# Second feed-forward product of a two-layer hybrid decoder trunk: one block product at a time over the whole depth, kept in PSUM, with the activations' operand sums made in stage one

## The chip, the core and the metric

The kernel runs on one core of a Trainium2 chip. Its time is the device time of one execution in microseconds (us). Three runs of the kernel before gave 3005.19, 3008.79 and 3010.06 us, a median of 3008.79. The execution that the profiler recorded took 3007.68 us, of which the profile's span covers 3005.6.

The engines are named as the profile names them: PE is TensorE, the matrix engine (PEld its weight loads), DVE is VectorE, ACT is ScalarE, POOL is GpSimd, SP is SyncE, which here issues all DMA transfers. PSUM is the memory in which PE accumulates, in eight banks of 128 x 512 f32; SBUF is the on-chip memory for everything else.

## The reference

Two layers. Each mixes three head groups (latent attention, a state space scan, a recurrent unit), attends to 256 memory tokens, and ends with a squared-ReLU feed-forward part. Only that part is changed:

```
DEPTH, SEQ, D_MODEL, D_FF = 2, 1024, 1024, 4096
hm = rms_norm(x, mlp_norm_g[l]) @ w_mlp1[l]          # (1024, 1024) @ (1024, 4096)
x  = x + jnp.square(jax.nn.relu(hm)) @ w_mlp2[l]     # (1024, 4096) @ (4096, 1024)
...
return rms_norm(x, final_norm_g)                     # after the last layer
```

Everything is f32. x is held transposed, as 8 tiles of 128 rows by 1024 tokens. An f32 product is formed from three: each operand is split into a high part, which ACT makes by a copy to fp32r, and a low part, which is the operand less its high part, and high x high, high x low and low x high are accumulated.

## The kernel before

Both feed-forward products go by Strassen's scheme in Winograd's form. A product of 2 x 2 blocks takes seven block products (M1, M2, M7, M5, M6, M4, M3 in the order of execution, `P_M1` to `P_M3` in the code) in place of eight, and pays with sums of blocks before and after. Block 11 of the result is M1 + M2, and the others are M1 with sums and differences of the rest. The weights' side of M7 and the following products is S3, S1, S2, A22 and S4, where S3 = A11 - A21, S1 = A21 + A22, S2 = A22 - S3, S4 = A12 - S2 (as the code forms them); the activations' side has the same chain of four sums.

**Stage one** (first product, `for f in range(1, NFP)`) goes through 15 pairs of hidden tiles after a first pair that is done plainly. A pair is seven products of 12 matmuls (L1514). For each pair SP loads four weight blocks (L627), ACT makes high parts (L1949), POOL makes low parts (L887) and the four weight sums (L893), DVE combines the seven results (L2548) and applies relu and the norm factor (`hidden`, L2486), ACT squares (L1937), and SP stores the four squared blocks of 128 x 512 (L632).

**Stage two** (second product) goes through seven panels of 512 hidden rows with all seven products each, and through an eighth panel plainly (16 units of 12 matmuls, L1605). A product of a panel is four units of six matmuls (L1588), and each unit fills one PSUM bank. Only M2 stays in PSUM, in banks 0 to 3, for all panels. The other six products of every panel go through banks 4 to 7, and DVE adds each of their units, 128 x 512, to accumulators in SBUF (`add_unit`, L2491: z1, z7, z5, z6, and x itself), so that the bank can be filled again. The operands of a product stand in one of four slots (`a_op`, `b_op`). To fill one, ACT makes the two high parts (L1976, L1989), DVE the activations' low part (L2510) and POOL the weights' low part (L922), each 128 x 1024; DVE also forms the activations' four sums of a panel (L2514) and POOL the weights' four (L927). Near the end POOL and DVE fold the accumulators together and into x (L974, L2596).

What sets the order is the order of the code on each engine, which is written out by hand. An engine goes through its own list and stops at each `wait_ge` until a semaphore has the number. PE waits for `x_add` (DVE has emptied the bank) and for `a_lo` and `b_lo` (the operands are there); ACT waits for `u_done` (PE is through with the slot) and for the sums.

Of the kernel before, what the change touches and what calls it, by code (L numbers as in the profile page):

```python
# [26 lines left out]
P = 128  # L27
DEPTH = 2
# [19 lines left out]
LAST = NFB - 1  # L48
# [7 lines left out]
W1_SUMS = 4 * (NFP - 1)  # L56
SLOTS = 4
FILL_SLOT = (0, 1, 2, 3, 0, 1, 2)
LATE_SLOT = (0, 1, 2, 3, 0, 2, 3)


def slot_of(b, i):

    return (LATE_SLOT if b == LAST - 1 else FILL_SLOT)[i]


def fills_done(b, i):

    return b * NPR + i + 1


def units_before(b, p):

    return (b * NPR + p) * 4


def slot_units(b, i):

    s = slot_of(b, i)
    before = [(bb, p) for bb in (b - 1, b) if bb >= 0 for p in range(NPR) if (bb, p) < (b, i) and slot_of(bb, p) == s]  # L80
    return units_before(*before[-1]) + 4 if before else None


def adds_before(b, p):

    x_products = (P_M4, P_M3)
    kept = sum((24 if m else 8) for m in range(b))
    return kept + 4 * sum(q != P_M2 and (b > 0 or q in x_products) for q in range(p))


PLAIN_A = ((0, 0), (0, 1), (2, 0), (2, 1))
PLAIN_B = ((1, 0), (3, 0), (1, 1), (3, 1))
PLAIN_B_ORDER = (0, 2, 1, 3)


def plain_units(slot):

    return max(units_before(LAST - 1, p) + 4 for p in range(NPR) if slot_of(LAST - 1, p) == slot)


def units_waited(n):

    return LAST * 24 + n - 19
# [4 lines left out]
LAST_ADDS = adds_before(LAST, 0)  # L108
LAST_UNITS = units_before(LAST, 0)
# [106 lines left out]
def x_tile(n):  # L216
# [51 lines left out]
def trunk(nc, xT, memT, posb, ropec, small, final_g, wt, wv, wh, lruw, outT):  # L268
# [10 lines left out]
    with ctx:  # L279
# [2503 lines left out]
```

## Time and profile before

| | us |
|---|---|
| median of three runs | 3008.79 |
| the profiled execution | 3007.68 |
| its span | 3005.6 |
| PE busy | 2824.3 (94%) |
| DVE busy | 1738.5 (58%) |
| POOL busy | 1596.1 (53%) |
| ACT busy | 1129.2 (38%) |
| stage one, two layers | 296.21 and 298.50 |
| stage two, two layers | 394.44 and 399.41 |

PE runs in order and is the busy engine nearly everywhere, so the span is what PE takes: its matmuls at their pitch, its idle time, and the stretches in which its granted clock is below 1.00. The busy time of a line counts overlapping matmuls once. In the rows, "idle before <- X" names the work whose end let the engine go on.

### The profile page before, as it was taken

How to read it: one execution, taken by the hardware profiler on the slowest of the kernel's cores; microseconds unless marked ns; L12 is line 12 of the kernel's file. 1: busy time of each engine (PE TensorE's matmuls, PEld its weight loads, DVE VectorE, ACT ScalarE, POOL GpSimd, SP SyncE). 2: the span in 40 equal slices, each digit the busy share in tenths (PEclk: the TensorE clock that was granted, in tenths of full speed). 3: DMA queues.
4: the chain of work that ended last, by engine and by line, in shares of the span. 5: the costliest groups of instructions: out<-in, count | busy, mean ns of one | idle time of the engine just before them, and what ended most of it. 6: DMA issues, size and time to landing. Idle time of an engine off the chain costs nothing.

```text
span 3005.6 us, 33919 instructions
## 1 busy us (share of the span) xinstructions
PE 2824.3 (94%) x12958; PEld 2192.6 (73%) x12958; DVE 1738.5 (58%) x1775; ACT 1129.2 (38%) x1762; POOL 1596.1 (53%) x897
## 2 busy tenths in 40 slices
PE   8999999999999988888999999999999999888887
PEld 6766668887788877666787566788787888766665
DVE  8574465034733357989776644630446333598987
ACT  3455543242433333222215655422414333422233
POOL 4334433422577776666633345234136777766666
PEclk9999999999999999999999999999999999999999
DMA  3100011310133342222110000113011333423221
GB/s 130 47 14 1 15 43 49 106 56 28 45 110 113 113 140 98 70 98 84 56 55 33 14 1 15 56 57 112 29 39 60 109 111 110 146 78 105 70 98 56
DMA packets 96298, 208.27 MB, mean 69 GB/s; under 512 B 11280, under 2 KB 13328, under 8 KB 95504
## 3 DMA queue, kind: packets, MB, share of 16 engines
q1 hardware_dynamic: 96144, 206.18, 20.3%
q8 instruction: 101, 1.65, 0.2%
q14 instruction: 53, 0.43, 0.0%
HBM read 168.13 MB, written 38.01 MB: 69 GB/s over the span
## 4 chain that ended last, share of the span: by engine, by line
PE 65%; DVE 20%; POOL 7%; ACT 3%; issue 2%; DMA 2%; SPq 0%; DVEq 0%; POOLq 0%; ACTq 0%
PE ps L1018 16%; PE ps L1514 12%; PE ps L1588 9%; PE ps L1386 6%; DVE raw_b L2514 6%; DVE b_op L2510 5%; PE ps L1240 4%; POOL ring L887 3%; PE ps L1270 2%; POOL raw L893 2%; PE ps L1442 2%; PE ps L1605 2%; PE ps L1466 2%; PE ps L1256 2%; DVE z L2491 2%
## 5 line engine op out<-in xcount | busy, mean ns | idle before, releaser
L1588 PE MATMUL ps<-b_op,a_op 128*128 128x512 f32 x2352 | 579.8, 409 | 109.0 <-DVE x L2491 59.2
L1588 PEld LDWEIGHTS ps<-b_op,a_op 128*128 128x128 f32 x2352 | 464.8, 199 | 223.7 <-DVE x L2491 64.2
L1018 PE MATMUL ps<-hA,wsp 128*128 128x512 f32 x1920 | 443.1, 392 | 0.1
L721 POOL TENSOR_TENSOR wsp<-raw,ones 128x1024 fp32r<-128x1024 f32 x63 | 125.9, 1999 | 570.8 <-PE ps L1018 454.9
L1018 PEld LDWEIGHTS ps<-hA,wsp 128*128 128x128 f32 x1920 | 360.3, 188 | 80.9 <-issue 6.2
L922 POOL TENSOR_TENSOR a_op<-raw_a,a_op 128x1024 fp32r<-128x1024 f32 x102 | 282.7, 2772 | 224.6 <-ACT a_op L1989 217.0
L887 POOL TENSOR_TENSOR ring<-raw,ring 128x512 fp32r<-128x512 f32 x210 | 272.9, 1299 | 150.4 <-ACT ring L1949 140.9
L1514 PE MATMUL ps<-hT,ring 128*128 128x512 f32 x1440 | 337.3, 394 | 16.1 <-POOL ring L887 16.1
L1514 PEld LDWEIGHTS ps<-hT,ring 128*128 128x128 f32 x1440 | 273.0, 190 | 76.7 <-POOL ring L887 19.5
L1976 ACT ACTIVATE b_op<-raw_b 128x1024 fp32r<-128x1024 f32 x98 | 103.5, 1056 | 424.3 <-DVE raw_b L2514 279.3
L1514 PE MATMUL ps<-hB,ring 128*128 128x512 f32 x1080 | 250.2, 389 | 0.8 <-POOL ring L887 0.8
L1949 ACT ACTIVATE ring<-raw 128x512 fp32r<-128x512 f32 x210 | 131.9, 630 | 274.7 <-POOL raw L893 205.0
L2510 DVE TENSOR_TENSOR b_op<-raw_b,b_op 128x1024 fp32r<-128x1024 f32 x98 | 219.2, 2247 | 26.3 <-ACT b_op L1976 26.2
L1514 PEld LDWEIGHTS ps<-hB,ring 128*128 128x128 f32 x1080 | 202.5, 188 | 43.6 <-issue 1.6
L927 POOL TENSOR_TENSOR raw_a<-raw_a,raw_a 128x1024 f32<-128x1024 f32 x56 | 181.5, 3241 | 4.4
L2514 DVE TENSOR_TENSOR raw_b<-raw_b,raw_b 128x1024 f32<-128x1024 f32 x56 | 182.7, 3263 | 1.0
L732 POOL TENSOR_TENSOR wsp<-raw,wsp 128x1024 fp32r<-128x1024 f32 x45 | 107.8, 2396 | 137.5 <-ACT wsp L1876 134.5
L1386 PE MATMUL ps<-hA,wsp 128*128 128x512 f32 x768 | 178.1, 391 | 0.8 <-ACT wsp L1876 0.7
L2280 DVE TENSOR_REDUCE nmx<-ps 128x1 f32<-128x256 f32 (+7 forms) x128 | 96.7, 757 | 132.9 <-PE ps L1243 130.9
L2548 DVE TENSOR_TENSOR mu<-mu,ps 128x512 f32<-128x512 f32 x90 | 61.8, 687 | 189.1 <-PE ps L1514 187.1
L724 POOL TENSOR_TENSOR wsp<-raw,wsp 128x1024 fp32r<-128x1024 f32 x63 | 166.2, 2638 | 4.9
L1386 PEld LDWEIGHTS ps<-hA,wsp 128*128 128x128 f32 x768 | 143.6, 188 | 32.7 <-issue 3.2
(326 smaller groups left out, 4592.4 us busy)
## 6 DMA issues: line engine op xcount, KB each, us to landing
raw<-in_weight_tiles SPq DMA_DIRECT2D x108, 512.0 KB, 3.3
hidden_tiles<-hm_s SPq DMA_DIRECT2D x128, 256.0 KB, 2.0
raw_a<-in_weight_tiles SPq DMA_DIRECT2D x64, 512.0 KB, 3.9
raw_b<-hidden_tiles SPq DMA_DIRECT2D x64, 512.0 KB, 5.4
raw<-in_weight_tiles SPq DMA_DIRECT2D x120, 256.0 KB, 3.1
outT<-x SPq DMA_DIRECT2D x16, 256.0 KB, 2.2
x<-in_xT SPq DMA_DIRECT2D x3, 1024.0 KB, 9.6
wh<-in_head_weights SPq DMA_DIRECT2D x8, 256.0 KB, 2.7
```

The lines of the kernel that those rows point to most:

```text
L721: pool.tensor_tensor(wsp[:, s, 0, :], raw[:, s, :], ones[:, 0:1].to_broadcast([P, TILE]), ALU.mult).then_inc(w_ready[s], 1)
L724: pool.tensor_tensor(wsp[:, s, 1, :], raw[:, s, :], wsp[:, s, 0, :].bitcast(F32), ALU.subtract).then_inc(w_ready[s], 1)
L887: pool.tensor_tensor(ring[:, FILL_SLOT[i], 1, :], blk(src), ring[:, FILL_SLOT[i], 0, :].bitcast(F32), ALU.subtract).then_inc(a_lo, 1)
L922: pool.tensor_tensor(op[:, 1, :, :], raw_t[:, :, :], op[:, 0, :, :].bitcast(F32), ALU.subtract).then_inc(a_lo, 1)
L927: pool.tensor_tensor(raw_a[out][:, :, :], raw_a[x0][:, :, :], raw_a[x1][:, :, :], op).then_inc(a_sum, 1)
L1018: last = pe.matmul(ps[:, 2 * buf + half, 0:n], w[:, k, col:col + P], rhs(part, k, half * n, n), start=(at_k == 0 and w is w_hi and part == 0),
L1386: last = pe.matmul(ps[:, 2 * (g % 2) + half, :], w[:, part, k, :], hA[:, a, k, half * HT:(half + 1) * HT], start=(k == 0 and part == 0 and ...
L1514: last = pe.matmul(ps[:, M_BANK[p], :], w[:, part, k, :], rhs(a, k), start=(k == 0 and part == 0 and a == 0), stop=(k == 3 and part == 1))
L1588: last = pe.matmul(ps[:, bank, :], w[:, part, q // 2, r, (q % 2) * P:(q % 2 + 1) * P], h[:, a, r, :], start=(r == 0 and part == 0 and a == ...
L1949: act.activation(ring[:, FILL_SLOT[i], 0, :], blk(src), ACT.Copy).then_inc(a_hi, 1)
L2510: dve.tensor_tensor(op[:, 1, :, :], raw_b[src][:, :, :], op[:, 0, :, :].bitcast(F32), ALU.subtract).then_inc(b_lo, 1)
L2514: dve.tensor_tensor(raw_b[out][:, :, :], raw_b[x0][:, :, :], raw_b[x1][:, :, :], ALU.subtract).then_inc(b_sum, 1)
```

## The change

Stage two is turned inside out. The loop over the seven products is now the outer one and the loop over panels the inner one, over all eight panels; there is no plain panel any more. A step n is one product of one panel, p, s = divmod(n, 8), and has 24 matmuls in four banks. All eight steps of a product accumulate in the same four banks: M1, M7, M6 and M3 in banks 4 to 7, M2, M5 and M4 in banks 0 to 3. Only when the eighth step is done does DVE add the 128 x 2048 result to the blocks of x that it belongs to (`block_add`; 13 such adds, and 4 of 128 x 512 for M3, `unit_add`). The accumulators z and the folds are gone. The last two steps of M3 are done bank by bank.

The operands come otherwise too. The activations' four sums are made in stage one, on DVE, from the squared blocks of a pair of 128 x 512 (`pair_sums`), and stored: seven blocks of each pair go to memory in place of four, three squared ones and four sums. Stage two loads the operand of a step as it is, 512 KB. The weights' sums move from POOL to DVE (`operand_sum`, one in each step of M7, M5, M6 and M3): a chain through kept blocks, for which a weight block of 512 KB is loaded in every step and two in those of M5, each in two transfers with runs of 256 columns. POOL makes the weights' low parts only. The four slots remain, and the last two steps have slots of their own.

At the start of stage one ACT makes the first two weight blocks' high parts ahead of the norm factor and of the four copies of `high_sums(0)`, which stood in front of them.

```diff
-                    for b in range(LAST):
-                        for p in range(NPR):
-                            panel_product(b, p)
+                    for n in range(RING_FILLS):
+                        p, s = step(n)
+                        operands_ready(n)
+                        if s == 0 and p == 0:
+                            pe.wait_ge(p1_kept, here(p1_kept, NFP - 1))
+                            pe.wait_ge(c_add, here(c_add, NPR * (NFP - 1) - 4))
+                            pe.wait_ge(hm_sq, here(hm_sq, 4 * NFP - 2))
+                        elif s == 0 and p == 1:
+                            pe.wait_ge(hm_sq, here(hm_sq, 4 * NFP))
+                        elif s == 0:
+                            pe.wait_ge(x_add, here(x_add, adds_before(p - 1)))
+                        for q in range(4):
+                            last = operand_products(n, q)
+                        last.then_inc(u_done, 1)
...
+                    def pair_sums(f):
+                        dve.wait_ge(hm_sq, here(hm_sq, 4 * f + 4))
+                        if f:
+                            dve.wait_ge(ht_st, here(ht_st, 64 * f))
+                        b11, b12, b21, b22 = (hms[k][:, cols_of(half)] for k in range(2) for half in range(2))
+                        dve.tensor_tensor(hts[0][:, :], b22, b12, ALU.subtract).then_inc(ht_sum, 1)
+                        dve.tensor_tensor(hts[1][:, :], b12, b11, ALU.subtract).then_inc(ht_sum, 1)
+                        dve.wait_ge(ht_sum, here(ht_sum, 4 * f + 2))
+                        dve.tensor_tensor(hts[2][:, :], b22, hts[1][:, :], ALU.subtract).then_inc(ht_sum, 1)
+                        dve.wait_ge(ht_sum, here(ht_sum, 4 * f + 3))
+                        dve.tensor_tensor(hts[3][:, :], b21, hts[2][:, :], ALU.subtract).then_inc(ht_sum, 1)
...
+                    def block_add(p, i):
+                        out, before = X_BLOCKS[p][i]
+                        bank = 4 * (1 - p % 2)
+                        dve.wait_ge(u_done, here(u_done, STEPS * (p + 1)))
+                        if before:
+                            dve.wait_ge(x_add, here(x_add, before))
+                        dve.tensor_tensor(out, ps[:, bank:bank + 4, :], out, ALU.add).then_inc(x_add, 1)
...
+                    for n in range(2, FILLS):
+                        if n + 1 < FILLS and step(n + 1)[0] in OPERAND_SUMS:
+                            operand_sum(n + 1)
+                        operand_low(n)
+                        p, i = step(n - SLOTS + 1 - STEPS)
+                        if n >= STEPS + SLOTS - 1 and i < X_ADDS[p]:
+                            block_add(p, i)
...
+                    for n in range(SLOTS, FILLS):
+                        sp.wait_ge(b_lo, here(b_lo, n - SLOTS + 1))
+                        load_hidden(n)
+                        sp.wait_ge(a_lo, here(a_lo, W1_FILLS + n - SLOTS + 1))
+                        if n == 6:
+                            sp.wait_ge(ht_st, here(ht_st, 64 * NFP))
+                        load_weights(n)
...
                     high_sums(2)
-                    high_sums(0)
-                    rstd_of(N_MLP, D, 4, rs[:, :]).then_inc(bc_done, 1)
                     w1_high(0, S_A11, 0)
                     w1_high(0, S_A12, 1)
+                    rstd_of(N_MLP, D, 4, rs[:, :]).then_inc(bc_done, 1)
+                    high_sums(0)
```

Three places show how the lists of the engines change. The first is DVE in stage one, from the last product of a pair to the middle of the next. Before (mu are the kept parts of the combination, ps are PSUM banks):

```order
L2548 TENSOR_TENSOR ps<-mu_54,ps 128x512
L2486 SCALAR_TENSOR_TENSOR ps<-ps,rs 128x512
L2548 TENSOR_TENSOR ps<-mu_54,ps 128x512
L2486 SCALAR_TENSOR_TENSOR ps<-ps,rs 128x512
L2548 TENSOR_TENSOR mu_54<-mu_54,ps 128x512
```

The same place after the change (hm_s are the squared blocks, hm_t the four sums):

```order
L2415 TENSOR_TENSOR ps<-mu_60,ps 128x512
L2346 SCALAR_TENSOR_TENSOR ps<-ps,rs 128x512
L2354 TENSOR_TENSOR hm_t_62<-hm_s_117,hm_s_116 128x512
L2355 TENSOR_TENSOR hm_t_63<-hm_s_116 128x512
L2357 TENSOR_TENSOR hm_t_64<-hm_s_117,hm_t_63 128x512
L2359 TENSOR_TENSOR hm_t_65<-hm_s_117,hm_t_64 128x512
L2415 TENSOR_TENSOR ps<-mu_60,ps 128x512
L2346 SCALAR_TENSOR_TENSOR ps<-ps,rs 128x512
```

Four sums have come between the last `hidden` of a pair and the first combination of the next.

The second place is SP's list for one pair of stage one. Before (hidden_tiles is the store in memory, raw the weight blocks):

```order
L627 DMA raw<-in_weight_tiles 128x512 x3
L632 DMA hidden_tiles<-hm_s_106 128x512
L627 DMA raw<-in_weight_tiles 128x512
L632 DMA hidden_tiles<-hm_s_107 128x512 x2
L632 DMA hidden_tiles<-hm_s_106 128x512
```

After:

```order
L612 DMA raw<-in_weight_tiles 128x512 x2
L623 DMA hidden_operands<-hm_t_62 128x512
L623 DMA hidden_operands<-hm_t_63 128x512
L623 DMA hidden_operands<-hm_t_64 128x512
L623 DMA hidden_operands<-hm_t_65 128x512
L612 DMA raw<-in_weight_tiles 128x512
L617 DMA hidden_operands<-hm_s_116 128x512
L612 DMA raw<-in_weight_tiles 128x512
L617 DMA hidden_operands<-hm_s_117 128x512 x2
```

The four stores of sums stand between the second and the third of the four weight loads.

The third place is DVE in the middle of stage two. Before, a part of one panel (z and x are the accumulators, raw_b the activations):

```order
L2491 TENSOR_TENSOR z_124<-ps,z_124 128x512 x2
L2510 TENSOR_TENSOR b_op_114<-raw_b_121,b_op_114 128x1024
L2510 TENSOR_TENSOR b_op_115<-raw_b_120,b_op_115 128x1024
L2514 TENSOR_TENSOR raw_b_120<-raw_b_123,raw_b_120 128x1024
L2491 TENSOR_TENSOR z_124<-ps,z_124 128x512 x2
L2510 TENSOR_TENSOR b_op_112<-raw_b_120,b_op_112 128x1024
L2514 TENSOR_TENSOR raw_b_122<-raw_b_122,raw_b_120 128x1024
L2491 TENSOR_TENSOR z_125<-ps,z_125 128x512 x2
```

After, three steps in M5 (raw_a and raw_c are the two weight blocks of a step):

```order
L2384 TENSOR_TENSOR raw_a_138<-raw_a_138,raw_c_146 128x1024
L2375 TENSOR_TENSOR b_op_127<-raw_b_145,b_op_127 128x1024
L2401 TENSOR_TENSOR x<-ps,x 128x4x512
L2384 TENSOR_TENSOR raw_a_139<-raw_a_139,raw_c_147 128x1024
L2375 TENSOR_TENSOR b_op_124<-raw_b_142,b_op_124 128x1024
L2401 TENSOR_TENSOR x<-ps,x 128x4x512
L2384 TENSOR_TENSOR raw_a_140<-raw_a_140,raw_c_148 128x1024
L2375 TENSOR_TENSOR b_op_125<-raw_b_143,b_op_125 128x1024
```

A step has one low part, one weight sum and, in few of them, one add of four banks, where a product of a panel had four adds of one bank each.

## Rows read from the trace of the kernel before

**Rows 1.** The page, part 1: busy time and share of each engine.

```profile
PE 2824.3 (94%) x12958; PEld 2192.6 (73%) x12958; DVE 1738.5 (58%) x1775; ACT 1129.2 (38%) x1762; POOL 1596.1 (53%) x897
```

**Rows 2.** Windows: stretch, length, PE, PEld, DVE, ACT, POOL busy, PEclk, DMA share, GB/s.

```profile
807.86:1104.07 296.21, 288.82 (x1260) 238.24 (x1261) 124.81 (x172) 107.59 (x189) 222.97 (x169) 0.98 0.35 118
1104.07:1498.51 394.44, 336.22 (x1369) 269.88 (x1368) 336.24 (x262) 120.06 (x130) 268.67 (x88) 0.93 0.24 80
2293.12:2591.62 298.50, 289.75 (x1260) 237.56 (x1261) 124.92 (x172) 107.97 (x189) 222.92 (x169) 0.99 0.35 118
2591.62:2991.03 399.41, 336.26 (x1370) 269.31 (x1369) 338.93 (x262) 126.74 (x144) 270.15 (x92) 0.94 0.22 76
```

**Rows 3.** Lines, stage two of layer 0: busy, mean ns, idle before, releasers.

```profile
L1588 PE MATMUL ps<-b_op,a_op 128*128 128x512 f32 x1176 | 291.1, 410 | 53.9 <-DVE x L2491 29.6 <-DVE z L2491 16.1 <-ACT hm_s L1937 7.9
...
L922 POOL TENSOR_TENSOR a_op<-raw_a,a_op 128x1024 fp32r<-128x1024 f32 x50 | 138.3, 2765 | 112.7 <-ACT a_op L1989 109.0 <-ACT a_op L2009 2.1
L2510 DVE TENSOR_TENSOR b_op<-raw_b,b_op 128x1024 fp32r<-128x1024 f32 x48 | 107.7, 2253 | 7.2 <-ACT b_op L1976 7.2
L2514 DVE TENSOR_TENSOR raw_b<-raw_b,raw_b 128x1024 f32<-128x1024 f32 x28 | 91.4, 3263 | 0.5
...
L2491 DVE TENSOR_TENSOR z<-ps,z 128x512 f32<-128x512 f32 x96 | 62.3, 683 | 16.5 <-PE ps L1588 16.1
L1976 ACT ACTIVATE b_op<-raw_b 128x1024 fp32r<-128x1024 f32 x48 | 50.7, 1056 | 212.8 <-DVE raw_b L2514 139.5 <-PE ps L1588 73.3
```

**Rows 4.** Timeline of stage two: start us, us, engine, line, operation, count, idle before.

```profile
1189.77 14.44 PE L1588 MATMUL ps<-b_op,a_op 128*128 128x512 f32 x63
...
1200.74 6.54 POOL L927 TENSOR_TENSOR raw_a<-raw_a,raw_a 128x1024 f32<-128x1024 f32 x2
1201.66 6.70 DVE L2514 TENSOR_TENSOR raw_b<-raw_b,raw_b 128x1024 f32<-128x1024 f32 x2
...
1209.14 16.65 PE L1588 MATMUL ps<-b_op,a_op 128*128 128x512 f32 x60 [4.93 <-DVE x L2491]
...
1221.97 1.22 DVE L2510 TENSOR_TENSOR b_op<-raw_b,b_op 128x1024 fp32r<-128x1024 f32 x1
```

**Rows 5.** DMA of stage two, layer 0: queue row, and KB each with us to landing.

```profile
q1 hardware_dynamic: 16144, 31.33, 23.8%
...
raw_b<-hidden_tiles SPq DMA_DIRECT2D x28, 512.0 KB, 5.4
```

**Rows 6.** DMA in 136.5 to 139.5 us, mostly head weights: packets, MB, share.

```profile
q1 hardware_dynamic: 688, 0.85, 89.4%
```

**Rows 7.** Timeline of the boundary from stage one to stage two, layer 0.

```profile
1117.56 7.75 PE L1588 MATMUL ps<-b_op,a_op 128*128 128x512 f32 x22 [7.88 <-ACT hm_s L1937]
```

**Rows 8.** Timeline of the start of stage one, layer 0.

```profile
820.47 13.70 PE L1514 MATMUL ps<-hT,ring 128*128 128x512 f32 x48 [6.90 <-POOL ring L887]
```

**Rows 9.** Timeline of one pair of stage one, layer 0.

```profile
1068.84 0.58 ACT L1937 ACTIVATE hm_s<-ps 128x512 f32<-128x512 f32 x1
1069.66 2.67 POOL L887 TENSOR_TENSOR ring<-raw,ring 128x512 fp32r<-128x512 f32 x2
...
1071.43 11.04 PE L1514 MATMUL ps<-hT,ring 128*128 128x512 f32 x48
...
1072.36 6.60 SPq L627 DMA_DIRECT2D raw<-in_weight_tiles  x3
...
1073.80 0.63 ACT L1949 ACTIVATE ring<-raw 128x512 fp32r<-128x512 f32 x1 [3.00 <-POOL raw L893]
...
1074.57 1.29 POOL L887 TENSOR_TENSOR ring<-raw,ring 128x512 fp32r<-128x512 f32 x1 [0.87 <-ACT ring L1949]
...
1079.00 0.43 SPq L632 DMA_DIRECT2D hidden_tiles<-hm_s  x1
...
1079.99 0.33 SPq L627 DMA_DIRECT2D raw<-in_weight_tiles  x1
```

**Rows 10.** The page, part 6: weight loads of stage one, us from issue to landing.

```profile
raw<-in_weight_tiles SPq DMA_DIRECT2D x120, 256.0 KB, 3.1
```

More of the change, by code:

```diff
@@ L55, with step, sums_done, loads_a @@
 W1_FILLS = NPR * (NFP - 1)
-W1_SUMS = 4 * (NFP - 1)
+FILL_SLOT = (0, 1, 2, 3, 0, 1, 2)
 SLOTS = 4
[L58 to L103, printed above, removed]
+STEPS = NFB
+FILLS = NPR * STEPS
+RING_FILLS = FILLS - 2
+OPERAND_SUMS = (P_M7, P_M5, P_M6, P_M3)
+X_ADDS = (4, 1, 2, 2, 3, 1, 4)
+def step(n):
+    return n // STEPS, n % STEPS
+def sums_done(n):
+    return sum(step(m)[0] in OPERAND_SUMS for m in range(n + 1))
+def loads_a(n):
+    return 32 * (n // SLOTS + 1 + sum(step(m)[0] == P_M5 for m in range(n % SLOTS, n + 1, SLOTS)))
+def slot_free(n):
+    return 0 if n >= RING_FILLS else n - SLOTS + 1
+def adds_before(p):
+    return sum(X_ADDS[:p])
 M_BANK = (4, 0, 5, 6, 7, 1, 2)
 T_PLACE = {2: 0, 0: 1, 1: 2, 3: 3}
-LAST_ADDS = adds_before(LAST, 0)
-LAST_UNITS = units_before(LAST, 0)
 NEG = -3.0e38
@@ new lines, in store_sums, with load_block @@
+                    def store_sums(f):
+                        for j, p in enumerate((P_M7, P_M5, P_M6, P_M4)):
+                            sp.wait_ge(ht_sum, here(ht_sum, 4 * f + j + 1))
+                            sp.dma_start(hm_d[layer, f, p, :, :], hts[j][:, :]).then_inc(ht_st, 16)
+                    def load_block(dst, n, rows, parity):
+                        t = 2 * R_MLP + 8 * step(n)[1] + 4 + 2 * (1 - rows)
+                        for c in range(2):
+                            tile = wt[layer, t + c, :, :].rearrange("p (k j m) -> p k j m", j=2, m=2 * P)
+                            sp.dma_start(dst[:, c, :].rearrange("p (k m) -> p k m", k=2), tile[:, :, parity, :])\
+                                .then_inc(blk_ready[n % SLOTS], 16)
@@ L661, in _ @@
                             load_first(f + 1, 0)
+                        else:
+                            sp.wait_ge(p_done, here(p_done, g1 + P_M1 + 1))
+                            sp.wait_ge(hm_st, here(hm_st, 48 * f))
+                            for n in range(2):
+                                load_weights(n)
+                                load_hidden(n)
+                        store_sums(f - 1)
+                        if more:
                             sp.wait_ge(a_lo, here(a_lo, g1 + S_A22 + 1))
@@ new lines, in _ @@
+                        store_hidden(f, 1, 1, P_M3, 2)
+                        store_hidden(f, 1, 0, P_M2, 3)
+                    sp.wait_ge(p_done, here(p_done, NPR * (NFP - 1)))
+                    for n in range(2, SLOTS):
+                        load_weights(n)
+                    sp.wait_ge(hm_st, here(hm_st, 48 * NFP))
+                    for n in range(2, SLOTS):
+                        load_hidden(n)
+                    store_sums(NFP - 1)
+                    sp.wait_ge(c_add, here(c_add, NPR * (NFP - 1)))
@@ L2543, in _, with unit_add @@
+                    def unit_add(q):
+                        dve.wait_ge(u_done, here(u_done, RING_FILLS + q + 1))
+                        dve.wait_ge(x_add, here(x_add, 10))
+                        out = x[:, 4 + q, HT:T]
+                        dve.tensor_tensor(out, ps[:, 4 + q, :], out, ALU.add).then_inc(x_add, 1)
                     for f in range(1, NFP):
```

566 lines of the change are left out of this document (169 added, 397 removed).

## The prediction

> **What bounds the kernel now.** I read the page's busy times first: PE is busy 94% of the span, every other engine under 60% [rows 1]. So only PE's waits, its slow clock and its number of matmuls can give time. Then the windows of the four stages that the change touches: in stage one PE is nearly always busy at a granted clock of 0.98 and 0.99; stage two takes 394.4 and 399.4 us, with 336 busy and the clock at 0.93 and 0.94 [rows 2]. The lost time is in stage two. The lines say what ends its waits: of 53.9 us idle before L1588 in layer 0, DVE's adds (L2491) end 45.7 and one square 7.9 [rows 3]. DVE is busy 336 of 394 us there [rows 2]: it is the engine that PE waits for, and the pages' average of 58% hides it.
>
> Why DVE is so full shows in the timeline. A low part of 128 x 1024 takes it 1.22 us when POOL is at rest, but two sums beside two adds of POOL take 6.70, and POOL's two take 6.54 [rows 4]. The two don't overlap: a pair takes 3.3 us, 1.2 of DVE and 2.1 of POOL. After that episode PE had stood for 4.93 us [rows 4]. The adds from PSUM show no such thing, 683 ns on the mean for 512 columns [rows 3]. The Trainium skill (SBUF — State Buffer, "SBUF: two separate sides") says that a DVE instruction with two SBUF inputs and a GpSimd one exclude each other for a whole instruction. The trace agrees, with the 6.70 beside the 6.54.
>
> **Pitch.** One matmul of 128 x 512 costs PE (14.44 - 11.04) / (63 - 48) = 0.2267 us [rows 4, 9]. A step of 24 is 5.44 us.
>
> **Stage two, the floor.** Before: 7 x 7 x 24 + 16 x 12 = 1368 matmuls, 310.1 us; the trace has 394.4 and 399.4, so 84 and 89 go to waits and to the slow clock behind them (0.07 x 394 = 28 us) [rows 2]. After: 56 x 24 = 1344 matmuls, 304.7 us. If PE never waits, the layers gain 89.7 and 94.7, together 184.4. Of this only 11 come from fewer matmuls.
>
> **Does anything hold PE in a step of 5.44 us?** Here I count each resource.
> - Banks: an add may start when its product's eight steps are done and is wanted eight steps (44 us) later. It is queued behind the low part of the 11th to 14th step after; that leaves two steps or more. The wait of rows 4 goes.
> - DVE: one low part, in 32 of 56 steps one sum, 13 adds of four banks. Not in the trace; between 2.1 us (2048 columns by the rate of 1.22 for 1024, less start) and 4 x 0.683 = 2.7 [rows 3]; I take 2.7. Per layer with the means of before, 2.253 and 3.263, that is 126 + 104 + 38 = 269 us of 305. In the densest stretch, the 24 steps of M7, M5 and M6, it is 24 x 5.52 + 5 x 2.7 = 146 us against 131 of PE. DVE would fall 15 us behind, and the ring lets it start three steps (16 us) ahead. But these means come from a POOL that had sums as well. Now POOL has one low part per step: 2 x 1.22 + 2.77 = 5.2 us even if nothing overlaps [rows 3, 4]. So DVE keeps up, and the sums do not hold PE.
> - POOL: 2.77 per step [rows 3]. ACT: two copies of 1.06. Both have room; the fill of a slot, 1.06 + 1.06 + 2.8 + one DVE operation, is done 6 us after PE leaves the slot, and PE comes back 16 us after.
> - DMA: 64 weight and 56 activation blocks of 512 KB, 62.9 MB per layer and not 31.3 [rows 5]: 206 GB/s, in M5 (three blocks a step) 289. At full share the queue moved 31.33 MB / (394.4 x 0.238) = 334 GB/s with 2 KB runs [rows 5]; with runs of 1 KB and less, 0.85 MB / (3.0 x 0.894) = 317 [rows 6]. M5 is tight but fits, and a block, issued when the low part of four steps before is done and wanted by the sum made two low parts ahead, has 8 us to land where it took 5.4 [rows 5]. SP issues up to five transfers a step at 0.43 each [rows 9], 2.2 us.
>
> The Trainium skill (DMA: Bandwidth & Descriptors, "Bandwidth") gives 138 GB/s for transfers of 64 KB and 341 for 1 MB, and would have transfers of a megabyte; the weights now come in pieces of 256 KB. No row here shows such pieces one after another at full rate.
>
> **Boundary from stage one to two.** Today PE stands 7.88 us there for a square that DVE's sums had delayed [rows 7]. Those sums go. But the loads of the third and fourth step may only start when stage one is over (their buffers lie on the squares' and its operands'), and the activations' ones wait for the last stores: two steps give 10.9 us; a square and a store some 4, a load 5.4 [rows 5], a fill 4. I expect a wait of 3 us per layer, bounds 0 and 8. Total +6.
>
> **Start of stage one.** PE stands 6.90 us for a weight block [rows 8], since POOL's `low_sums(0)` comes late behind the norm factor. With two high parts moved ahead, POOL does its first lows and sums while the norm is computed. I take 3 of the 6.9 us per layer, bounds 0 and 6.9: -6.
>
> **The four sums in stage one.** They are on DVE, which has time (125 of 296 us busy [rows 2]). What they cost is POOL's time: each has two SBUF inputs and keeps POOL out for half of 1.22, 0.6 us. They start when the last square of the pair is done, at 1069.42 in rows 9, which is when POOL starts its two lows for M7 and M5. POOL's low for M7 ends at 1071.0 and PE wants it by 1071.2; the low for M6 ends at 1075.86 and PE wants it at 1071.43 + 2 x 2.72 - 0.2 = 1076.7 [rows 9]. Three or four delays of 0.6 make it some 1.5 late against a slack of 0.8: 0.7 us of PE per pair. Behind DVE's sums are queued its next combination and `hidden`, 4 us late; ACT's square of M2 comes as late, and just in time.
>
> There is a longer loop. The last weight load of a pair now waits in SP behind four stores (4 x 0.43), and the next pair's POOL chain starts with it: landing 3.1 [rows 10], high part 0.7, eight POOL operations at 1.335 (2.67 / 2) = 10.7, three collisions 1.8, the high part of S2 0.9, SP's issues 2.8. Sum 20.0 us, and 20.4 if a megabyte of stores ahead of it delays the landing by 0.4; the pair is 84 x 0.2267 = 19.04 long. I take 20.2, +1.2 us per pair, 14 pairs, two layers: +34. Bounds: 0 (no exclusion, slack holds) and +50 (20.8).
>
> By the skill's rule on the two engines the sum keeps these 34 us; without the rule it would have 0 in their place.
>
> **Sum.** 3007.7 - 184.4 + 6 - 6 + 34 = 2857, against the profiled execution, 1.1 below the median of the three runs.
>
> **Rivals.**
> - A, stage one gives no cost: DVE's sums fall into POOL's gaps (it is busy 223 of 296 us [rows 2]). 2857 - 34 = 2823. Against it: the sums start at the one point where POOL runs without a gap.
> - B, transfers become the bound in stage two: half rate, 167 GB/s, for 256 KB pieces. A step of 1.05 MB takes 6.3 us and one of M5, 1.57 MB, 9.4; 48 x 0.85 + 8 x 4.0 = 73, less the lead of 16, 57 us per layer: 2857 + 114 = 2971. For it: twice the bytes; against it: rows 6.
> - C, the other side. Each block's landing is waited for in turn and the ring hides nothing: 120 blocks at 5.4 us [rows 5] are 648 us a layer in place of 304.7: 2857 + 2 x 343 = 3543. It decides from 7.1 us of transfer per step (397 / 56) on. Against it: four buffers, and loads issued as soon as a low part is done.
> - D, the waits don't go but change their cause (a slot is filled late by POOL, or the sums' chain delays DVE at each product), half of the 84 us stays: 2857 + 84 = 2941.
>
> **How the numbers follow.** Forecast with its own spread 2835 to 2885: 0.63. A 0.13, B 0.11, D 0.09, C 0.04. The range takes in A and the milder half of B: 2820 to 2910, with 0.19 outside. Within 0.2% (6 us, what a measurement can tell) nothing of this lies, 0.01; slower 0.03; faster 0.96.
>
> **What would show it.** In the profile after: stage two 305 to 312 us per layer with PE busy throughout, the clock at 1.00, no wait on DVE's adds, and one short wait at the third step; DVE near 230 us there. Stage one 10 to 20 us longer, with short waits of PE on POOL's ring before M7 and M6, and POOL's low parts at 1.9 us in two of seven. Wrong if stage two is above 320 us, if stage one is as long as before, or if PE waits on transfers.

## The result and the profile after

| | us, median (lowest to highest) | ratio to before, 95% |
|---|---|---|
| before, the same chip, 4 runs | 3007.54 (3005.19 to 3010.06) | |
| after, 4 runs | 2924.19 (2920.84 to 2932.03) | 0.9726 (0.9705 to 0.9748) |

The change is worth 83 us; the prediction had 151. The profiled execution took 2932.03 us, the longest of the four and 8 us over their median; its span is 2930.3 us against 3005.6 before. So the stage times below, which are this execution's, are together some 8 us long. Read first the windows of the same four stages, in the columns of [rows 2]:

```profile
806.54:1149.58 343.04, 300.41 (x1262) 235.42 (x1260) 209.03 (x240) 111.48 (x192) 230.12 (x166) 0.98 0.38 131
1149.58:1461.40 311.82, 307.13 (x1345) 253.88 (x1344) 213.90 (x117) 118.27 (x118) 153.63 (x59) 0.99 0.63 204
2253.99:2602.96 348.97, 303.03 (x1261) 237.41 (x1260) 209.00 (x241) 111.44 (x192) 230.06 (x166) 0.97 0.37 129
2602.96:2915.98 313.02, 308.36 (x1347) 254.50 (x1346) 204.93 (x113) 123.57 (x132) 152.56 (x63) 0.99 0.62 200
```

Against [rows 2], stage two lost 82.6 and 86.4 us, together 169.0, and stage one gained 46.8 and 50.5, together 97.3. 75.3 us is the whole difference of the spans, so 3.6 us came from the rest. Stage two gained nearly what was forecast; stage one gave back more than half of it.

**Stage two.** The lines of layer 0 (busy, mean ns, idle before), which answer to [rows 3]:

```profile
L1513 PE MATMUL ps<-b_op,a_op 128*128 128x512 f32 x1344 | 307.3, 391 | 4.7 <-POOL a_op L917 4.7
...
L2375 DVE TENSOR_TENSOR b_op<-raw_b,b_op 128x1024 fp32r<-128x1024 f32 x55 | 74.2, 1350 | 89.8 <-ACT b_op L1894 89.8
...
L2388 DVE TENSOR_TENSOR kept_a<-raw_a,kept_a 128x1024 f32<-128x1024 f32 x16 | 48.1, 3006 | 0.0
...
L2401 DVE TENSOR_TENSOR x<-ps,x 128x2048 f32<-128x2048 f32 x13 | 29.7, 2283 | 0.0
```

The 53.9 us of idle time before the matmuls are 4.7. A low part on DVE takes 1.35 us on the mean in place of 2.25, and DVE stands 89.8 us idle for ACT's copies: it is ahead now, not behind. PE's timeline has one wait in the stage, at its third step:

```profile
1149.58 11.04 PE L1513 MATMUL ps<-b_op,a_op 128*128 128x512 f32 x48
1165.31 296.27 PE L1513 MATMUL ps<-b_op,a_op 128*128 128x512 f32 x1296 [4.69 <-POOL a_op L917]
```

The other 1296 matmuls run without a gap. The wait of [rows 7], 7.88 us for a square, is gone; the one at the third step, 4.69 us for a weight block's low part, has come in its place. The transfers, too, hold: the densest stretch, in M5, and the queue of the whole stage:

```profile
1265.00:1308.00 43.00, 43.00 (x192) 35.61 (x191) 35.98 (x19) 16.10 (x16) 19.45 (x8) 1.00 0.85 275
```

```profile
q1 hardware_dynamic: 49655, 63.38, 62.5%
...
raw_b<-hidden_operands SPq DMA_DIRECT2D x54, 512.0 KB, 3.7
raw_a<-in_weight_tiles SPq DMA_DIRECT2D x96, 256.0 KB, 3.3
```

PE is busy for all of the 43 us with 275 GB/s behind it.

**Stage one.** PE's timeline of two pairs of layer 0, in the middle of the stage:

```profile
957.18 11.33 PE L1458 MATMUL ps<-hT,ring 128*128 128x512 f32 x48 [1.41 <-POOL ring L882]
968.35 5.60 PE L1458 MATMUL ps<-hB,ring 128*128 128x512 f32 x24
974.86 3.01 PE L1458 MATMUL ps<-hB,ring 128*128 128x512 f32 x12 [0.91 <-POOL ring L882]
979.28 11.33 PE L1458 MATMUL ps<-hT,ring 128*128 128x512 f32 x48 [1.41 <-POOL ring L882]
```

This pair takes 979.28 - 957.18 = 22.10 us where 84 matmuls are 19.04. PE waits for POOL's low parts, but POOL's work alone doesn't fill the pair: it is busy 230 of 343 us. The chain of waits shows what it hangs on, in order of time (start, us, what):

```profile
968.22 4.43 DMA raw<-in_weight_tiles
...
972.73 0.64 ACT ring L1867
...
977.62 1.62 POOL ring L882
...
979.31 1.63 POOL ring L882
...
981.00 1.63 POOL raw L888
...
983.49 1.30 POOL ring L882
...
984.86 1.30 POOL raw L888
...
990.75 4.00 DMA raw<-in_weight_tiles
```

From one landing of a fourth weight load, 968.22 + 4.43 = 972.65, to the end of POOL's eighth operation, 984.86 + 1.30 = 986.16, are 13.5 us. From there to the issue of the next fourth load, at 990.75, SP is the reason:

```profile
980.95 5.61 SPq L612 DMA_DIRECT2D raw<-in_weight_tiles  x2
986.60 2.49 SPq L623 DMA_DIRECT2D hidden_operands<-hm_t  x4
989.14 0.80 SPq L612 DMA_DIRECT2D raw<-in_weight_tiles  x1
989.98 0.72 SPq L617 DMA_DIRECT2D hidden_operands<-hm_s  x1
990.75 0.46 SPq L612 DMA_DIRECT2D raw<-in_weight_tiles  x1
```

The second load goes out at 986.23. The fourth could go at 988.9, where POOL's low part for its block ends, but the four stores stand ahead of it and of the third. An issue here takes 0.62 to 0.80 us, where [rows 9] have 0.33 and 0.43. Then the load lands after 4.0 us here, 4.4 in the pair before, and not 3.1. So this loop is 13.5 + 4.6 + 4.0 = 22.1 us.

This pair is at one edge of what the others show. I took the same three stretches for the fourteen fourth loads of each layer from the trace. From the landing to the issue of the next second load it is 13.6 us in nearly all. From there to the issue of the fourth load it is 4.1 us in the median (3.9 to 4.7 in layer 0), where this pair has 4.5. The landing takes 4.5 us on the mean in layer 0 (3.9 to 5.2) and 5.0 in layer 1 (3.9 to 7.4), where this pair has 4.0. That gives 22.2 and 22.7 us. The kernel before has 2.7 us between the second load's issue and the fourth's, and its fourth loads land after 3.3 us in layer 0 and 3.8 in layer 1 in the median; the 3.1 of [rows 10] is the median over all four loads of a pair.

**The start of stage one** became longer. [Rows 8] have the first M7 at 820.47, 12.6 us after the first matmul of the stage at 807.86; now it is 16.95 (806.54 to 823.49):

```profile
806.54 2.88 PE L1458 MATMUL ps<-hB,ring 128*128 128x512 f32 x12
814.53 4.83 PE L1458 MATMUL ps<-hB,ring 128*128 128x512 f32 x12 [5.10 <-ACT hm_s L1855]
823.49 6.80 PE L1458 MATMUL ps<-hT,ring 128*128 128x512 f32 x18 [4.14 <-POOL ring L882]
```

The wait of 6.90 on POOL is 4.14, as meant, but a new one of 5.10 stands before it. DVE's sixteen operations of this place show why:

```profile
790.08 23.06 DVE L2330 SCALAR_TENSOR_TENSOR hTf<-x,sm,hTf 128x512 f32<-128x512 f32 x16
```

### The profile page after: what moved, and what is told of

It reads as the page before. It is cut to its first block, busy times and chain, and to the rows that moved or that the text cites. A ratio compares the mean times of both kernels' runs of the same rounds, so it can differ in the third digit from the quotient of the medians.

```text
span 2930.3 us, 33643 instructions
## 1 busy us (share of the span) xinstructions
PE 2791.1 (95%) x12910; PEld 2158.4 (74%) x12910; DVE 1645.5 (56%) x1599; ACT 1128.2 (38%) x1742; POOL 1390.7 (47%) x839
## 4 chain that ended last, share of the span: by engine, by line
PE 66%; POOL 13%; DVE 7%; DMA 6%; ACT 4%; issue 2%; SPq 2%; POOLq 0%; ACTq 0%; DVEq 0%
PE ps L1513 20%; PE ps L962 17%; POOL ring L882 7%; PE ps L1330 6%; POOL raw L888 5%; DMA raw<-in_weight_tiles 5%; PE ps L1184 4%; PE ps L1214 2%; PE ps L1386 2%; PE ps L1410 2%; PE ps L1200 2%; PE ps L1078 2%; PE ps L1345 2%; PE ps L1361 1%; DVE hTf L2330 1%
## 5 line engine op out<-in xcount | busy, mean ns | idle before, releaser
L1513 PE MATMUL ps<-b_op,a_op 128*128 128x512 f32 x2688 | 615.5, 391 | 9.3 <-POOL a_op L917 9.3
L1513 PEld LDWEIGHTS ps<-b_op,a_op 128*128 128x128 f32 x2688 | 508.0, 189 | 116.4 <-POOL a_op L917 10.2
L882 POOL TENSOR_TENSOR ring<-raw,ring 128x512 fp32r<-128x512 f32 x210 | 291.1, 1386 | 219.2 <-ACT ring L1867 210.0
L1458 PE MATMUL ps<-hB,ring 128*128 128x512 f32 x1080 | 264.8, 400 | 44.1 <-POOL ring L882 33.9
L1894 ACT ACTIVATE b_op<-raw_b 128x1024 fp32r<-128x1024 f32 x112 | 118.7, 1060 | 349.7 <-PE ps L1513 326.5
L2375 DVE TENSOR_TENSOR b_op<-raw_b,b_op 128x1024 fp32r<-128x1024 f32 x112 | 150.8, 1346 | 180.5 <-ACT b_op L1894 180.4
L917 POOL TENSOR_TENSOR a_op<-kept_a,a_op 128x1024 fp32r<-128x1024 f32 x64 | 168.4, 2635 | 163.2 <-ACT a_op L1899 162.7
L917 POOL TENSOR_TENSOR a_op<-raw_a,a_op 128x1024 fp32r<-128x1024 f32 x48 | 119.3, 2485 | 141.8 <-ACT a_op L1899 141.8
L888 POOL TENSOR_TENSOR raw<-raw 128x512 f32<-128x512 f32 x120 | 166.7, 1389 | 9.4
L962 PE MATMUL ps<-hB,wsp 128*128 128x512 f32 x672 | 155.2, 391 | 2.1 <-DVE x L2249 2.1
```

Of the source, the lines that this page charges most:

```text
L882: pool.tensor_tensor(ring[:, FILL_SLOT[i], 1, :], blk(src), ring[:, FILL_SLOT[i], 0, :].bitcast(F32), ALU.subtract).then_inc(a_lo, 1)
L888: pool.tensor_tensor(blk(out), blk(a), blk(b), op).then_inc(a_sum, 1)
L917: pool.tensor_tensor(op[:, 1, :, :], source_a(n)[:, :, :], op[:, 0, :, :].bitcast(F32), ALU.subtract)\
L962: last = pe.matmul(ps[:, 2 * buf + half, 0:n], w[:, k, col:col + P], rhs(part, k, half * n, n), start=(at_k == 0 and w is w_hi and part == 0),
L1458: last = pe.matmul(ps[:, M_BANK[p], :], w[:, part, k, :], rhs(a, k), start=(k == 0 and part == 0 and a == 0), stop=(k == 3 and part == 1))
L1513: last = pe.matmul(ps[:, 4 * (1 - p % 2) + q, :], w[:, part, q // 2, r, (q % 2) * P:(q % 2 + 1) * P], h[:, a, r, :], start=(s == 0 and r = ...
```

## The experiments

The gain of stage two was as forecast, so what was open was stage one (the place of the stores on SP, their bytes, DVE's sums, the order at the start), and which part of the change gives stage two's gain. All medians are of four or five executions, and each ratio is to the kernel before on the same chip. What was expected speaks of theories by number: "theory 1" has the four stores' place in SP's list as the larger part of stage one's loss, "theory 2" DVE's four sums; 1a and 1b part the stores' effect into SP's issues and their bytes.

**late**: the changed kernel, with the stores of the sums behind the fourth weight load (the first added line is for the last pair, which loads nothing for a next one).

```diff
-                        store_sums(f - 1)
+                            store_sums(f - 1)
                         if more:
                             sp.wait_ge(a_lo, here(a_lo, g1 + S_A22 + 1))
                             load_first(f + 1, 3)
                         store_hidden(f, 0, 0, P_M1, 1)
                         if more:
                             sp.wait_ge(a_lo, here(a_lo, g1 + S_S4 + 1))
                             load_first(f + 1, 1)
+                            store_sums(f - 1)
```

> The changed kernel with one move: SP's four stores of sums go behind the fourth weight load of the pair instead of ahead of the third. Theory 1 (the fourth weight load is issued late, behind the four stores, and lands late among them; the next pair's chain begins with it): the pair of stage one falls from 22.3 us to 19.7 (19.3 to 20.2), the time from 2924 to about 2852 us (2838 to 2865). Theory 2 (DVE's four sums keep POOL out, and that alone makes the pair long): pair 21.5 us or more, time 2905 us or more.

Measured 2870.77 us (2867.45 to 2872.45), ratio 0.9551 (0.9535 to 0.9567): 53 us less than the changed kernel, with no byte and no sum taken away. So the place is the larger part; the forecast of 2852 was 19 us too low, and the time lies outside its 2838 to 2865. In the chain of waits the fourth loads of three pairs now start 20.1 us apart, each as soon as POOL's last low part of the pair ends:

```profile
954.08 3.81 DMA raw<-in_weight_tiles
...
972.86 1.29 POOL ring L883
...
974.17 3.69 DMA raw<-in_weight_tiles
...
994.18 3.96 DMA raw<-in_weight_tiles
```

The landing is 3.8 us on the mean in this layer, between before's 3.4 and the changed kernel's 4.5; the stores now follow the load at once, and later, below, tests that. SP now needs 2.7 us from the second load to the fourth, as before the change.

**start**: the changed kernel, with ACT's order at the start of stage one as before.

```diff
+                    high_sums(0)
+                    rstd_of(N_MLP, D, 4, rs[:, :]).then_inc(bc_done, 1)
                     w1_high(0, S_A11, 0)
                     w1_high(0, S_A12, 1)
-                    rstd_of(N_MLP, D, 4, rs[:, :]).then_inc(bc_done, 1)
-                    high_sums(0)
```

> The changed kernel with ACT's old order at the start of stage one (high_sums(0) and the norm factor ahead of the first two weight blocks' high parts). Theory: with POOL's first lows and sums moved ahead they fall on DVE's sixteen sum_of operations, which took 23.1 us instead of 14.8; undone, the stretch from the first pair product to M7 goes from 17.0 back to 12.6 us, 4.4 per layer: 2915 us. Rival (the move does help, as I predicted, and the stretch is longer for the stores or DVE's four sums): 2924 to 2930 us, stretch 17 us or more.

Measured 2922.19 us (2919.57 to 2925.92), ratio 0.9724 (0.9708 to 0.974), where 2915 was expected: no difference from the changed kernel that can be measured. The mechanism is there, though. DVE's sixteen operations and the first M7 in its timeline:

```profile
788.79 14.82 DVE L2330 SCALAR_TENSOR_TENSOR hTf<-x,sm,hTf 128x512 f32<-128x512 f32 x16
```

```profile
805.81 5.72 PE L1458 MATMUL ps<-hB,ring 128*128 128x512 f32 x24 [0.39 <-POOL ring L882]
818.43 10.58 PE L1458 MATMUL ps<-hT,ring 128*128 128x512 f32 x36 [6.90 <-POOL ring L882]
830.53 3.01 PE L1458 MATMUL ps<-hT,ring 128*128 128x512 f32 x12 [1.52 <-POOL ring L882]
```

They take 14.82 us and not 23.06, and M7 starts 12.62 us after the first matmul. But a wait of 1.52 follows at once, and the loop of the pairs sets the pace from there: stage one of layer 0 is 340.5 us long, not 343.0, so of 4.3 us won 1.8 are lost again behind M7. What is won ahead of a loop that is longer than PE's work is partly waited away behind it. (Layer 1 can't be compared in this way: its stage one is 9.6 us shorter than in the changed kernel's profiled execution, which was the long one.)

**late_start**: both edits.

> Both moves at once: stores of sums behind the fourth weight load, and ACT's old order at the start of stage one. If the two causes are separate the gains add: 2924 - 72 - 9 = 2843 us (2828 to 2858). Theory 2 of the pair's length: 2895 us or more.

Measured 2868.11 us (2865.28 to 2871.46), ratio 0.954 (0.9524 to 0.9556), 2.7 below late and again 25 above what was expected: with a pair of 20 us the loop still sets the pace.

**b_sums**: the kernel before, with the four sums of a pair on DVE added for 14 of the 16 pairs, at their new place, and nothing stored. Stage two is as before.

```diff
+                        dve.tensor_tensor(hts[0][:, :], b22, b12, ALU.subtract).then_inc(ht_sum, 1)
+                        dve.tensor_tensor(hts[1][:, :], b12, b11, ALU.subtract).then_inc(ht_sum, 1)
...
+                        dve.tensor_tensor(hts[2][:, :], b22, hts[1][:, :], ALU.subtract).then_inc(ht_sum, 1)
...
+                        dve.tensor_tensor(hts[3][:, :], b21, hts[2][:, :], ALU.subtract).then_inc(ht_sum, 1)
```

> The kernel before with DVE's four sums of a pair added in stage one for 14 of the 16 pairs, not stored and not used; all else as before. Theory 1: the sums alone cost 0.3 to 0.8 us per pair in 13 pairs of each layer, 3007 + 8 to 21 us. Theory 2: they cost the whole 3.3 us, 3007 + 85 = 3092 us.

Measured 3029.3 us (3027.65 to 3030.55), ratio 1.0076 (1.0059 to 1.0093): the sums alone cost 22 us, a little over the 8 to 21 expected. Fourth loads are issued at 970.40 and 989.89, 19.49 us apart, and land after 3.2.

**b_early, b_late, b_tiny**: b_sums with the four stores too. In b_early they are where the changed kernel has them, in b_late behind the fourth load, and in b_tiny at the early place, but each stores 8 of its 512 columns.

What b_early adds to b_sums on SP, where the second load is behind and the third ahead:

```diff
+                    def store_sums(f):
+                        for j in range(4):
+                            sp.wait_ge(ht_sum, here(ht_sum, 4 * f + j + 1))
+                            sp.dma_start(ht_d[layer, f, j, :, :], hts[j][:, :]).then_inc(ht_st, 16)
...
+                            store_sums(f - 1)
```

The line that b_tiny has in place of b_early's:

```diff
-                            sp.dma_start(ht_d[layer, f, j, :, :], hts[j][:, :]).then_inc(ht_st, 16)
+                            sp.dma_start(ht_d[layer, f, j, :, 0:8], hts[j][:, 0:8]).then_inc(ht_st, 16)
```

> The kernel before with DVE's four sums of a pair (14 of 16 pairs) and with their four stores of 256 KB in SP's list ahead of the third weight load, as in the changed kernel; stage two untouched. Theory 1 (the stores' place makes the pair long, in any kernel): pair 22.3 us instead of 19.04, time 3007 + 26 x 3.2 = 3090 us (3075 to 3100). Rival (the length comes from something else in the changed kernel, such as its buffers' addresses): pair below 20.5 us, time below 3050 us.

> The same with the four stores behind the fourth weight load. Theory 1: pair 20.05 us as in the changed kernel with that move, time 3007 + 10 + 26 x 1.0 = 3043 us (3032 to 3050). Rival: no difference to the stores in the early place, 3090 us.

> As the kernel with the stores in the early place, but each store takes 8 of the 512 columns (the rest isn't stored), so that SP issues as much and moves next to nothing. If SP's issues make the fourth load late (theory 1a), the pair stays near 21.3 us, time 3065 us; if the stores' bytes ahead of and beside the loads do (theory 1b), the pair is 19.6 us, time 3033 us.

| on top of before | us, median | ratio (95%) | over before, us |
|---|---|---|---|
| b_sums: sums | 3029.30 | 1.0076 (1.0059 to 1.0093) | 22 |
| b_late: sums, stores late | 3038.19 | 1.0108 (1.0091 to 1.0125) | 31 |
| b_tiny: sums, tiny stores early | 3050.87 | 1.0150 (1.0133 to 1.0167) | 44 |
| b_early: sums, stores early | 3095.14 | 1.0298 (1.0281 to 1.0315) | 88 |

b_early and b_late came out as expected. b_tiny lies halfway between its two values, 3033 and 3065: issues and bytes both count. The 88 us of b_early are what stage one of the changed kernel pays apart from its start (97.3 - 2 x 4.3 = 88.7). They are now taken apart: sums 22, four more issues ahead of the loads 22, the bytes at that place 44; at the late place bytes and issues together cost 9. A part of how the bytes cost is in SP's timelines. b_tiny, then b_early, the same place of one pair:

```profile
992.85 1.85 SPq L641 DMA_DIRECT2D sum_tiles<-hm_t  x4
994.75 0.43 SPq L629 DMA_DIRECT2D raw<-in_weight_tiles  x1
995.22 0.43 SPq L634 DMA_DIRECT2D hidden_tiles<-hm_s  x1
995.70 0.43 SPq L629 DMA_DIRECT2D raw<-in_weight_tiles  x1
```

```profile
985.32 2.62 SPq L641 DMA_DIRECT2D sum_tiles<-hm_t  x4
988.00 0.76 SPq L629 DMA_DIRECT2D raw<-in_weight_tiles  x1
988.81 0.63 SPq L634 DMA_DIRECT2D hidden_tiles<-hm_s  x1
989.48 0.46 SPq L629 DMA_DIRECT2D raw<-in_weight_tiles  x1
```

With small stores the run from the first store to the fourth load is 2.85 us here, with whole ones 4.16. In these two pairs the fourth load lands after 3.90 and 4.05 us, which is hardly a difference, but other pairs show one. The chains of waits of the next loads, b_tiny first:

```profile
1016.45 3.67 DMA raw<-in_weight_tiles
```

```profile
1011.35 5.21 DMA raw<-in_weight_tiles
...
1034.32 4.73 DMA raw<-in_weight_tiles
```

The medians of the fourteen fourth loads, where two values are given for layer 0 and layer 1:

| | second load's issue to fourth's, us | landing of the fourth, us |
|---|---|---|
| before | 2.7 | 3.3 and 3.8 |
| b_sums | 2.7 | 3.3 and 3.6 |
| b_late | 2.7 | 3.7 and 4.0 |
| b_tiny | 3.2 | 3.7 and 3.8 |
| b_early | 4.2 | 4.4 and 4.5 |

So the bytes act on both: SP's issues behind them take 1.0 us more a pair, and the landing 0.7 us more. Together that is some 48 us in 28 pairs, near the 44 measured. Why an issue takes longer with bytes queued ahead, no run shows. That the landing is a little longer with tiny stores than in b_sums goes with a third load and a square's store issued more closely ahead of the fourth; I did not test that by itself.

**b_nosum**: the kernel before, without the four activation sums that DVE makes per panel in stage two (that part of the computation is left out; the waits stay).

```diff
-                        dve.tensor_tensor(raw_b[out][:, :, :], raw_b[x0][:, :, :], raw_b[x1][:, :, :], ALU.subtract).then_inc(b_sum, 1)
+                        dve.sem_inc(b_sum, 1)
```

> The kernel before without DVE's four sums per panel in stage two (the unsummed blocks are used in their place); nothing else changed, the adds of every unit stay. Theory 3 (the sums, which exclude POOL's, are what made DVE late with the adds): stage two falls from 394 to about 325 us, time about 2867 us (2850 to 2890). Rival (the adds of every unit with their four banks hold PE whatever DVE's load): stage two 370 us or more, time 2960 us or more.

Measured 2879.84 us (2876.73 to 2881.3), ratio 0.9582 (0.9566 to 0.9598), 13 above what was expected and inside its 2850 to 2890. Its window and PE's line of stage two, layer 0:

```profile
1100.08:1430.97 330.89, 315.65 (x1370) 258.23 (x1368) 253.02 (x234) 122.18 (x130) 263.81 (x88) 0.99 0.28 95
```

```profile
L1588 PE MATMUL ps<-b_op,a_op 128*128 128x512 f32 x1176 | 270.1, 391 | 12.3 <-DVE z L2491 7.3 <-ACT hm_s L1937 3.1 <-POOL a_op L922 1.9
```

394.44 has become 330.89, 63.6 of the 82.6 us that the whole change takes from this stage, with the clock at 0.99. So taking the activation sums from DVE is by itself enough for three quarters of the gain, with every add of a unit left in place; all the rest adds 19 us: 24 matmuls fewer (5.4), the products kept in PSUM, the weights' sums elsewhere. Since DVE's and POOL's sums hold each other up, taking away POOL's alone might bring much of the same time; no run did that, and so the three quarters are not a share that belongs to DVE's sums only.

**dve_twice**: the changed kernel, with each low part of DVE in stage two made twice.

```diff
+                        dve.tensor_tensor(op[:, 1, :, :], raw_b[n % SLOTS][:, :, :], op[:, 0, :, :].bitcast(F32), ALU.subtract)\
+                            .then_inc(twice, 1)
+                        dve.wait_ge(twice, here(twice, n + 1))
```

> The changed kernel with every low part of DVE in stage two made twice (56 more operations of 1.1 us or more per layer). My forecast said that DVE has room in a step: then stage two stays at 312 to 316 us and the time at 2924 to 2932 us. If DVE bounds stage two after the change, it grows by 56 x 1.2 = 67 us per layer: 3050 us or more.

Measured 2943.5 us (2942.76 to 2951.24), ratio 0.9802 (0.9787 to 0.9817): 19 us more than the changed kernel, above what plain room would give and far below what a bound would. Windows of stage two, layer 0:

```profile
1150.66:1469.53 318.87, 308.35 (x1344) 254.07 (x1345) 312.25 (x169) 116.57 (x115) 185.35 (x59) 0.99 0.62 199
```

DVE is busy 312 of 319 us, 98 more than in the changed kernel, and the stage is 7 us longer. DVE is thus not the bound of the changed kernel; some 90 us of room are there. Most of the 7 us are at the edges: a boundary wait of 6.4 in place of 4.7, and one of 2.5 before the last step, both for DVE's low parts. (The two profiled executions are 12 us apart, the medians 19; the former is the changed kernel's long one.)

**later, later_start**: the stores of late moved one place further, behind the second square's store (the edit is shown against late); and that with the order of start.

```diff
                             load_first(f + 1, 1)
-                            store_sums(f - 1)
                         store_hidden(f, 1, 1, P_M3, 2)
+                        if more:
+                            store_sums(f - 1)
                         store_hidden(f, 1, 0, P_M2, 3)
```

> The stores of sums one place further down than behind the fourth weight load: behind the store of the second square. Theory 1b (bytes of these stores slow the landing of the fourth load, 3.7 to 4.0 us instead of 3.1): the load lands in 3.1, the pair falls from 20.05 to 19.5 us, time 2857 us (2850 to 2864). Rival (what is left of the pair's length is the exclusion of POOL by DVE's sums alone, or the sums now wait for their stores to land): 2868 us or more.

> The same with ACT's old order at the start of stage one, which was worth 2 to 3 us in the two comparisons before: 2854 us, or 2866 if the further place brings nothing.

later measured 2865.18 us (2862.41 to 2865.35), ratio 0.9532 (0.9519 to 0.9545), against late's 0.9551 (0.9535 to 0.9567): likely a little faster, between the two values expected. Both theories have a part in that. The fourth load's landing falls from late's 3.8 us to 3.4 or 3.5 in the median. But DVE's sums now wait for the landing of their own last stores in nine of the 28 pairs. The waits of layer 0 (us in total, times, longest):

```profile
DVE hm_t L2356 <- DMA hidden_operands<-hm_t: 12.7, 4, 4.1
```

The pairs that begin with the longest of these waits, 3.9 us and more (two in later, one in later_start), take 21.7 us where most take 19.3 to 20.0. So the place furthest down is not free either.

later_start measured 2857.28 us (2856.46 to 2860.56), ratio 0.951 (0.9497 to 0.9523). It is the fastest, 149 us under the kernel before on its chip and 67 under the changed one, and 3 above the 2854 expected. Windows of its two stages, layer 0:

```profile
807.94:1117.51 309.57, 295.49 (x1261) 235.44 (x1262) 208.06 (x233) 110.06 (x190) 236.24 (x169) 0.98 0.43 145
1117.51:1428.65 311.14, 307.18 (x1345) 253.87 (x1344) 213.54 (x117) 118.32 (x118) 153.70 (x59) 0.99 0.64 204
```

The landing is back at 3.5 us in the median, most pairs take 19.3 to 20.0 (PE's M7 starts at 944.35, 963.92 and 983.77), and PE's waits before these M7 are under 0.4 us. Here the old order at the start pays: later_start is 8 us under later on the same chip, where start had brought 2. What is left over before, 309.57 - 296.21 = 13.4 us, is nearly all in the pairs: from the first M7 to the last are 283 us, against 270 in the kernel before.

## Why the prediction was wrong, and where it was right

The changed kernel came out 75 us above the forecast (profiled execution 2932.03 against 2857), 14 above the range's end by the median. The sum, term by term:

| term | forecast, us | measured, us |
|---|---|---|
| stage two, both layers | -184.4 + 6 | -169.0 |
| start of stage one | -6 | +8.6 |
| rest of stage one, 28 pairs | +34 | +88.7 |
| the other stages | 0 | -3.6 |

Some 8 of the 75 us are the profiled execution's own, above its median.

- **Stage two: right.** The floor, 304.7, was met to 7 and 8 us; PE runs through, no wait on DVE's adds, clock 0.99, DVE at 214 where 230 was forecast. The stage lasts 311.8 and 313.0 us where 305 to 312 were named, the second just outside. The reason was right too: b_nosum gets three quarters of the gain without DVE's sums, and dve_twice shows that DVE has room now. The mechanism that the forecast named, DVE and POOL kept apart when both read SBUF, is seen again. The Trainium skill (SBUF — State Buffer, "SBUF: two separate sides") has the one that starts first hold the ports for its whole instruction, while the other is blocked. The trace agrees in the main: a sum of 0.69 us alone takes 1.66 beside POOL. But two contested operations, one of each engine, are through every 1.69 us (POOL's start at 977.62, 979.31 and 981.00), where 0.69 + 1.30 = 1.99 would be the time if nothing overlapped. Here the measurement decides: a small part of the two does overlap.
- **Boundary: right in place, 3 us per layer short.** The wait on the third step was 4.69 us where 3 stood. Of the 7.1 us over the floor the other 2.4 are behind it, where the granted clock was 0.81 (1162 to 1180).
- **Start of stage one: wrong sign.** The step that failed is "POOL does its first lows and sums while the norm is computed. I take 3 of the 6.9 us". I looked at what POOL would gain, and not at who works beside it: DVE's sixteen operations read SBUF at that time, and POOL's early work stretched them from 14.82 to 23.06 us (a single one from 0.74 to 1.77, with DVE never idle between them), as start and its 14.82 show. It is the same exclusion on which the rest of the prediction was built.
- **The pairs of stage one: the loop was the right one, two of its terms were too small.** The forecast's "longer loop" is the chain that the profile shows, and the rival that stage one costs nothing is out: b_sums alone has 22 us. The steps that failed are its last two terms. The terms against the trace: high parts, POOL's eight operations and the collisions 14.1, measured 13.6 (a collision costs POOL 0.33 us and not 0.6). "SP's issues 2.8", measured 4.1 in the median (4.6 in the pair shown above). "Landing 3.1", or 3.5 behind the stores, measured 4.5 on the mean in layer 0 and 5.0 in layer 1 (4.0 in the pair shown). Together 22.2 and 22.7, and not 20.4, and I had taken 20.2: 2.0 us in the 14 pairs of layer 0 and 2.5 in those of layer 1 are 63 us, which covers this row's 55. Two readings lie behind this. The issue time was read from [rows 9], where no stores stand close ahead, and multiplied; behind a megabyte of stores it is 0.45 to 0.80. And 3.1 is the median of all four loads of a pair, while the fourth, the one in the loop, took 3.3 and 3.8 in the kernel before already; the 0.4 added for the stores came out as more than 1. None of the forecast's three signs of being wrong came true: they watch stage two, and stage one only for being too short.
- **Transfers in stage two (rival B): out.** PE has no wait in M5, the densest part. Here the Trainium skill (DMA: Bandwidth & Descriptors, "Bandwidth"), which asks for transfers of about a megabyte, did not decide: with many 256 and 512 KB transfers in flight the queue moved 275 GB/s at a share of 0.85, which by my estimate is 275 / 0.85 = 323 at full share. The rival that the waits only change their cause (2941) is near in time, but wrong in kind: stage two had no such waits. The slower case (3543) is out.
- **The range.** The bound of 20.8 us for a pair, +50, rested on the same issue time and the same landing as the value, and so the error went through both at once; the pairs took +88.7. The range's upper end, 2910, was wider only for the milder half of rival B, which has nothing to do with stage one.

## What to carry to other kernels

When loads that a loop waits for share a queue with stores, work out the loop from the landing of one load to the landing of the next, and place whatever isn't waited for behind the last load that is: moving four stores behind two loads was worth 53 us, nearly two thirds of what the whole change brought. A price read where a queue is idle is a lower bound where stores stand ahead. Read such a loop in many of its turns and not in one: here a single pair had the landing too short and the issues too long. And when work of one engine is moved earlier, look at who works beside it there: here DVE's operations that read SBUF became 8 us longer.

## What the runs showed of the hardware

- The time that SP takes to issue a transfer goes with the bytes that are queued: the same four stores took 1.85 us in most pairs of b_tiny and 2.1 to 2.6 in b_early, and the load behind them 0.43 and mostly 0.45 to 0.85.
- A contested operation of 128 x 512 costs the two engines unequally: POOL 1.63 us in place of 1.30, DVE 1.66 in place of 0.69. A steady DVE stream of sixteen such beside POOL grew by more than half, 14.82 to 23.06.
- A fourth weight load of 256 KB lands in 3.3 us in the median of layer 0 without the stores of sums (b_sums), in 3.7 with tiny ones ahead or whole ones behind (b_tiny, b_late), and in 4.4 with whole ones ahead (b_early); the longest of the changed kernel took 5.2 in layer 0 and 7.4 in layer 1.
